# Gathering rows for the experts without their reciprocal root, and the first gather by bank

## What is computed

```python
hn = rms_norm(x, norm2_g[i])                       # x * rsqrt(mean(x*x) + eps) * g, row by row
x  = x + hier_moe(hn, ...)
# hier_moe: group = argmax(hn @ w_rg + b); two best of the 8 experts in that group, by hn @ w_re + b
#   for each expert e, its rows xb:  hdn = silu(xb @ w_gate[e]) * (xb @ w_up[e]);  y = hdn @ w_down[e]
#   x[row] += gate_weight[row, e] * y
```

## Time and profile before

| what | us |
|---|---|
| median of 3 runs | 1759.47 (1758.72 to 1763.71) |
| the profiled execution | 1758.96 |
| its span, first to last instruction | 1756.9 |
| first gather to the end of the experts, layer 0 | 435.7 to 880 |
| the same in layer 1 | 1307.6 to 1751 |

### The profile page before, as it was taken

How to read it: one execution, slowest core, us unless ns; L and a number is a source line. 1 busy time by engine, 2 the same in 40 slices (tenths; PEclk the granted TensorE clock), 3 DMA queues, 4 the chain that set the end, 5 groups by cost and what they waited for, 6 DMA issues and landing times.

```text
span 1756.9 us, 23311 instructions
## 1 busy us (share of the span) xinstructions
PE 1696.4 (97%) x9006; PEld 1062.0 (60%) x9006; DVE 719.3 (41%) x1341; ACT 683.0 (39%) x1541; POOL 667.5 (38%) x536
## 2 busy tenths in 40 slices
PE   8999999999999999899999999999999999998997
PEld 5889877787434444343378898777874444443443
DVE  5728788624222212121266387876241212222122
ACT  5565787754211111111156567877541111111111
POOL 6888776894000000000077987768930000000000
PEclk9999999999999999999999999999999999999999
DMA  6554312766999999999954452227569999999997
GB/s 252 209 184 153 144 49 102 291 278 239 365 417 425 427 426 426 426 425 428 414 223 161 180 192 97 94 100 313 220 250 413 427 426 425 426 426 427 426 423 303
DMA packets 52708, 528.48 MB, mean 301 GB/s; under 512 B 5704, under 2 KB 8520, under 8 KB 22384
## 3 DMA queue, kind: packets, MB, share of 16 engines
q1 hardware_dynamic: 52560, 526.89, 73.5%
q0 software_dynamic: 32, 0.02, 0.0%
HBM read 525.82 MB, written 1.06 MB: 300 GB/s over the span
## 4 chain that ended last, share of the span: by engine, by line
PE 65%; DMA 11%; DVE 9%; SPq 5%; ACT 4%; issue 3%; POOL 2%; DVEq 0%; ACTq 0%
PE PS L1274 18%; DMA view<-in_w_exp_down_dram 11%; PE PS L1303 9%; PE PS L858 8%; PE PS L860 8%; PE PS L859 8%; SPq L682 5%; DVE view L1954 5%; PE PS L1221 2%; POOL view L2321 2%; PE PS L1207 1%; PE PS L1065 1%; DVE view L1950 1%; PE PS L833 1%; ACT view L1527 1%
## 5 line engine op out<-in xcount | busy, mean ns | idle before, releaser
L2321 POOL TENSOR_TENSOR view<-view,view 128x512 fp32r<-128x512 f32 x448 | 579.1, 1316 | 555.9 <-DVE view L1856 466.8
L1274 PE MATMUL PS<-view,view 128*64 128x512 f32 x2048 | 454.6, 596 | 24.1 <-issue 23.3
L1415 ACT ACTIVATE view<-view 128x512 fp32r<-128x512 f32 x448 | 273.7, 630 | 152.8 <-PE PS L860 147.7
L1274 PEld LDWEIGHTS PS<-view,view 128*64 128x64 f32 x2048 | 153.6, 137 | 296.8 <-issue 293.5
L858 PE MATMUL PS<-view,view 128*128 128x512 f32 x704 | 285.2, 405 | 5.7 <-POOL view L2321 3.2
L860 PE MATMUL PS<-view,view 128*128 128x512 f32 x704 | 274.9, 390 | 0.0
L859 PE MATMUL PS<-view,view 128*128 128x512 f32 x704 | 274.7, 390 | 0.0
L1303 PE MATMUL PS<-view,stb 128*64 128x512 f32 x1024 | 230.3, 597 | 9.3 <-DMA view<-in_w_exp_down_dram 6.5
L2221 DVE SCALAR_TENSOR_TENSOR view<-PS,gcol,view 128x512 fp32r<-128x512 f32 x64 | 48.0, 750 | 447.6 <-ACT view L1723 447.5
L858 PEld LDWEIGHTS PS<-view,view 128*128 128x128 f32 x704 | 132.3, 188 | 33.5 <-issue 5.9
L1303 PEld LDWEIGHTS PS<-view,stb 128*64 128x64 f32 x1024 | 72.2, 136 | 132.6 <-issue 116.6
(11 more groups left out here) (254 smaller groups left out, 2034.5 us busy)
## 6 DMA issues: line engine op xcount, KB each, us to landing
view<-in_w_mix_dram SPq DMA_DIRECT2D x56, 2048.0 KB, 7.6
view<-in_w_exp_up_dram SPq DMA_DIRECT2D x54, 2048.0 KB, 27.6
view<-in_w_exp_gate_dram SPq DMA_DIRECT2D x50, 2048.0 KB, 28.2
view<-in_w_exp_down_dram SPq DMA_DIRECT2D x50, 2048.0 KB, 30.4
view<-in_w_exp_down_dram SPq DMA_DIRECT2D x44, 512.0 KB, 14.9
view<-in_w_exp_up_dram SPq DMA_DIRECT2D x28, 512.0 KB, 15.3
view<-in_w_exp_gate_dram SPq DMA_DIRECT2D x14, 1024.0 KB, 12.4
view<-in_w_exp_gate_dram SPq DMA_DIRECT2D x28, 512.0 KB, 25.9
```

The costliest lines, as they stand in the source:

```text
L1274: ins = pe.matmul(bank(ph, name, j)[e * CAP:(e + 1) * CAP, :], xgT1[:, k, at + e * CAP:at + (e + 1) * CAP], rows8(expert_block(j, kind, e) ...
L1415: nc.scalar.activation(highs(chunk), weights(slot8, chunk), ACT.Copy).then_inc(*high_ready.up(ph))
L2321: g_.tensor_tensor(weights(low8, chunk), weights(slot8, chunk), highs(chunk), ALU.subtract).then_inc(*low_ready.up(ph))
```

## The change

- ACT writes XNh as X rounded, without the root, one half of the columns at a time: columns 0 to 511 of both tiles after its work for n = 0, columns 512 to 1023 after its work for n = 1. The squares of n = 0 and 1 go to other scratch memory, since XNh now lies where they went.
- DVE writes the low part of columns 0 to 511 into a tile of its own, xl0, after n = 0; that of columns 512 to 1023 into XNl after `select(0)`; and once more that of columns 0 to 511 into XNl after the gates' weights, for the later gathers. Each is one tensor_tensor of 2 x 512 columns.
- The first gather runs bank by bank, 8 products each: banks 0 and 1 ahead of the gate product, bank 2 ahead of its k = 2, bank 3 ahead of its k = 4.
- `roots` makes the root of each place: a product of the selection (128 stationary columns, fp32) with the roots of the rows, one moving column, for two pairs and two tiles, so four products. For the first half they run ahead of the gate product into bank 4, for later halves behind the place weights in `turned_selection` of the odd pair before. ACT copies them to `rcol`.
- silu gets the root's column as its scale, and DVE's multiplication of up and silu becomes a scalar_tensor_tensor with the same column.
- The further passes get the same in their own form (not shown).

```diff
-        xnh_ready = sig("xnh_ready", 1, 0)
-        xnl_ready = sig("xnl_ready", TT, 0)
+        xnh_ready = sig("xnh_ready", 2, 0)
+        xnl_ready = sig("xnl_ready", 3, 0)
@@ PE, gather and first_gather
                     if i == 0:
                         pe.wait_ge(*S_ready.at(ph, h + 1))
+                        pe.wait_ge(*xnl_ready.at(ph, 3))
...
-                def first_gather(i, t, part):
-
+                def first_gather(i):
+
+                    pe.wait_ge(*xnh_ready.at(ph, 1 + i // 2))
+                    pe.wait_ge(*xnl_ready.at(ph, 1 + i // 2))
+                    pe.wait_ge(*free(ph, "xg", 0, i))
                     for k in (2 * i, 2 * i + 1):
...
+                        cols = slice(k * P, (k + 1) * P)
+                        for t in range(TT):
+                            for lower in range(2):
+                                rows = (xl0 if lower and i < 2 else XNl if lower else XNh)[:, t, cols]
+                                ins = pe.matmul(bank(ph, "xg", 0, i)[:, (k % 2) * HALF:(k % 2 + 1) * HALF],
+                                                rows, S2[0][:, t, :], start=(t == 0 and not lower),
+                                                stop=(t == TT - 1 and lower == 1))
+                    ins.then_inc(*fill(ph, "xg", 0, i))
+
+                def roots(o, h):
+
+                    for j in (2 * h, 2 * h + 1):
+                        at = (j % 2) * 2 * CAP
+                        for t in range(TT):
+                            ins = pe.matmul(o[:, j % 2:j % 2 + 1], S2[h % 2][:, t, at:at + P].bitcast(F32),
+                                            st[:, 64 + t:65 + t], start=(t == 0), stop=(t == TT - 1))
                     return ins
...
                 pe.wait_ge(*S_ready.at(ph, 1))
...
+                first_gather(0)
+                first_gather(1)
+                pe.wait_ge(*free(ph, "rc"))
+                roots(bank(ph, "rc"), 0).then_inc(*fill(ph, "rc"))
...
+                    if gathered(j):
+                        ins = roots(PS[:, 7, TT * P + 2:TT * P + 4], h + 1)
                     ins.then_inc(*fill(ph, "G", j))
...
                         for k in range(KD):
+                            if kind == 0 and j == 0 and k in (2, 4):
+                                first_gather(1 + k // 2)
                             if kind == 0 and j % 2 == 0 and k % 2 == 0:
                                 pe.wait_ge(*out_of(ph, "xg", h, k // 2))
@@ ACT
...
-                act.wait_ge(*r_ready.at(ph, 1))
-                act.wait_ge(*sumsq.made(ph))
-                for t in range(TT):
-                    ins = nc.scalar.activation(XNh[:, t, :], X[:, t, :], ACT.Copy, scale=st[:, 64 + t:65 + t])
-                ins.then_inc(*xnh_ready.up(ph))
+                    nc.scalar.activation(XNh[:, :, n * COLS:(n + 1) * COLS], X[:, :, n * COLS:(n + 1) * COLS], ACT.Copy
+                                         ).then_inc(*xnh_ready.up(ph))
...
-                for i in (0, 2):
-                    gathered_out(0, i)
...
+                gathered_out(0, 0)
+                roots_out(("rc",), bank(ph, "rc")[:, 0:2], rcol[:, 0:2])
+                gathered_out(0, 2)
...
-                nc.scalar.activation(silug, PS[:, 0, :], ACT.Silu).then_inc(*drain(ph, "g", j))
+                nc.scalar.activation(silug, PS[:, 0, :], ACT.Silu, scale=rcol[:, j % 4:j % 4 + 1]
+                                     ).then_inc(*drain(ph, "g", j))
@@ ACT, selection_out
+                if gathered(j):
+                    at = (j + 1) % 4
+                    ins = nc.scalar.activation(rcol[:, at:at + 2], PS[:, 7, TT * P + 2:TT * P + 4], ACT.Copy)
@@ DVE
+                def lower_rows(to, n, high_rows):
+
+                    cols = slice(n * COLS, (n + 1) * COLS)
+                    dve.wait_ge(*xnh_ready.at(ph, high_rows))
+                    v.tensor_tensor(to, X[:, :, cols], XNh[:, :, cols], ALU.subtract).then_inc(*xnl_ready.up(ph))
...
+                    if n == 0:
+                        lower_rows(xl0, 0, 1)
...
                 select(0)
-                dve.wait_ge(*xnh_ready.at(ph, 1))
-                for t in range(TT):
-                    v.scalar_tensor_tensor(out=XNl[:, t, :], in0=X[:, t, :], scalar=r_row[:, t:t + 1],
-                                           in1=XNh[:, t, :], op0=ALU.mult, op1=ALU.subtract
-                                           ).then_inc(*xnl_ready.up(ph))
+                lower_rows(XNl[:, :, COLS:], 1, 2)
...
                 gates()
+                lower_rows(XNl[:, :, 0:COLS], 0, 1)
...
-                v.tensor_tensor(hh, PS[:, 1, :], silug, ALU.mult).then_inc(*drain(ph, "u", j))
+                v.scalar_tensor_tensor(out=hh, in0=PS[:, 1, :], scalar=rcol[:, j % 4:j % 4 + 1], in1=silug,
+                                       op0=ALU.mult, op1=ALU.mult).then_inc(*drain(ph, "u", j))
```

More of the change, by code:

```diff
@@ L233, in unit_fills @@
 def unit_fills():
-    f = [(("xg", k), 5 + k % 3) for k in range(KD)]
+    f = [(("xg", k), 5 + k % 3) for k in range(KD)] + [(("rc",), 4)]
     for j in range(PAIRS):
@@ L374, in encoder @@
         XNh = view(r_w, TT, D, dt=F32R)
+        xl0 = view(r_v, TT, COLS, dt=F32R)
         sq = view(r_w, 2 * D)
@@ L1233, in first_gather @@
+                def roots(o, h):
[4 more added lines that the diff above has]
+                                            st[:, 64 + t:65 + t], start=(t == 0), stop=(t == TT - 1))
                     return ins
-                pe.wait_ge(*xnh_ready.at(ph, 1))
                 pe.wait_ge(*S_ready.at(ph, 1))
-                for i in range(4):
-                    pe.wait_ge(*free(ph, "xg", 0, i))
-                    for t in range(TT):
-                        first_gather(i, t, XNh)
@@ L1241, in first_pass @@
-                pe.wait_ge(*xnl_ready.at(ph, 1))
-                for i in range(4):
-                    first_gather(i, 0, XNl)
-                pe.wait_ge(*xnl_ready.at(ph, 2))
-                for i in range(4):
-                    first_gather(i, 1, XNl).then_inc(*fill(ph, "xg", 0, i))
+                first_gather(0)
+                first_gather(1)
+                pe.wait_ge(*free(ph, "rc"))
+                roots(bank(ph, "rc"), 0).then_inc(*fill(ph, "rc"))
                 def turned_selection(j):
@@ L1343, in unit @@
                     ins.then_inc(*fill(ph, "xg", k))
+                pe.wait_ge(*free(ph, "rc"))
+                for j in range(PAIRS):
+                    for t in range(TT):
+                        ins = pe.matmul(bank(ph, "rc")[:, j:j + 1], S[:, t, j * P:(j + 1) * P].bitcast(F32),
+                                        st[:, 64 + t:65 + t], start=(t == 0), stop=(t == TT - 1))
+                ins.then_inc(*fill(ph, "rc"))
                 for k in range(KD - 2, KD):
@@ L1632, in layer @@
                         act.wait_ge(*out_of(ph, "wo", n, t))
-                        nc.scalar.activation(sq[:, (2 * n + t) * COLS:(2 * n + t + 1) * COLS],
-                                             X[:, t, n * COLS:(n + 1) * COLS], ACT.Square,
+                        if n:
+                            act.wait_ge(*sumsq.at(ph, 14 + t))
+                        nc.scalar.activation(stb[:, :] if t else Lms[1], X[:, t, n * COLS:(n + 1) * COLS], ACT.Square,
                                              accum_out=small[:, 2 * n + t:2 * n + t + 1]).then_inc(*sumsq.up(ph))
@@ L1652, in gathered_out, with roots_out @@
                     ins.then_inc(*drain(ph, "xg", h, i))
-                for i in (0, 2):
-                    gathered_out(0, i)
+                def roots_out(key, rows, to):
+                    act.wait_ge(*full(ph, *key))
+                    nc.scalar.activation(to, rows, ACT.Copy).then_inc(*drain(ph, *key))
+                    act.wait_ge(*out_of(ph, *key))
+                gathered_out(0, 0)
+                roots_out(("rc",), bank(ph, "rc")[:, 0:2], rcol[:, 0:2])
+                gathered_out(0, 2)
                 act.wait_ge(*soft.at(ph, 4))
@@ L1744, in unit @@
                     scaled(ph, xgT[:, k, :], ("xg", k), G2 + k)
+                act.wait_ge(*full(ph, "rc"))
+                nc.scalar.activation(rcol[:, :], bank(ph, "rc")[:, 0:4], ACT.Copy).then_inc(*drain(ph, "rc"))
+                act.wait_ge(*out_of(ph, "rc"))
                 for j in range(PAIRS):
```

8 lines of the change are left out of this document (2 added, 6 removed).

## The result

Medians of 12 runs of each kernel on the same chip:

| what | before, us | changed, us |
|---|---|---|
| median | 1760.47 (1758.43 to 1763.71) | 1765.52 (1762.78 to 1767.43) |
| ratio, 95% interval | | 1.0028 (1.0020 to 1.0035) |
| the profiled execution | 1758.96 | 1766.88 |
| its span | 1756.9 | 1764.9 |

What follows compares the result with a forecast made beforehand. The prediction took the weight stream at 426 GB/s to bound the expert stage, its start set by the release behind pair 0's down product. It added +0.78 us a layer: 1758.96 + 2 x 0.78 = 1760.5 us, range 1757.0 to 1763.8.

Steps and rivals of the forecast that it cites:

- the sum: Path from first gather to pair 0's down product: 1.95 + 0.84 + 2.30 + 0.06 = 5.15 against 4.37, +0.78 us a layer.
- T: Point in the expert stage where the weight stream gets going for good: 464.7, set by the release at 463.34.
- theory F: From the follow-ups, not the prediction: TensorE's 3.49 us stand in layer 1's first transposes is instruction fetch, some 4.2 us in all.
- what I haven't seen, 0.01: Chance 0.01 kept for causes not named, with no place or size; counted under faster.
- B's one hand-off: TensorE stops once a layer inside the gate product for a bank's copy, 1.14 us: 1762.8.
- D: Roots and bank 0's copy hold the first gate product to 440.1: 1.6 us more a layer, 1763.7; chance 0.03.
- the release term: Load behind pair 0's down product released at 464.1 instead of 463.34: +0.78 us a layer.
- The earlier loads: First quarter load 1.8 us earlier in the gate product, twelve loads ending at 462.7, not 464.7; gain ends as idle queue.
- The rest of the hiding: ACT's and DVE's moved copies lie beside other work at no cost; tightest is bank 3's copy, 0.8 us in hand.
- rival B: TensorE waits for bank copies inside the gate product: 1762.8 for one a layer, 1767.3 for all three; chance 0.12.
- The roots' price: Eight records ahead of the gate product, 0.087 us each, upper bound 0.122: 0.70 to 0.98, middle 0.84 taken.
- The base: Profiled execution of the kernel before, 1758.96 us, to which 2 x 0.78 was added.

Runs made afterwards that it cites:

- the place put back: Changed kernel plus 91 instructions in a branch never executed, layer 1's first instruction back at place 18 of 256: 1761.22 us (1.0011); repeated, 1761.56 (1.0007).
- the place moved alone: Kernel before plus 165 instructions in a branch never executed, layer 1's first instruction moved from place 18 to 183: 1764.56 us, 1.0033.
- hold ahead of pair 0's down product: Kernel before with ten short keep-busy products (2.2 us) ahead of pair 0's down product in each layer, place kept: 1762.95 us, 1.0017.
- hold behind the first gather: Kernel before with ten short keep-busy products between the first gather and pair 0's gate product, place kept: 1762.42 us, 1.0017.
- the three products: Three bf16 products in the wait ahead of the last row transposes, place 18: kernel before 1758.60 us (0.9996), repeated 1758.93 (0.9995); changed kernel 1759.58 (1.0000).

## Why the prediction was wrong

**The failed step** is the one that isn't in the sum. I priced every instruction that is executed on the way to T and between pairs, and held the rest of the program for unchanged. TensorE's program is 165 instructions longer ahead of the target of a jump that is taken 445 us behind the first gather, and by theory F a block's end came to lie 14 instructions behind that target. That stand, with the slower clock behind it, is 4.2 us in the profiles (431.50 - 427.34), 4.3 by the runs with the place put back (1765.52 - 1761.22, medians of two comparisons with their own kernel before; by the ratios to it, 1.0028 less 1.0009, 3.3), and 5.4 by the runs with the place moved alone (1764.56 - 1759.16). It was among "what I haven't seen, 0.01". None of the rivals had it; that B's one hand-off and D end near 1763 is chance.

**The sum itself.** With the place put back, the change costs +1.6 us (1.0009; 2.1 and 2.5 by the medians), and +1.56 was forecast. That the two agree so well is partly luck: two of the sum's parts were off, with opposite signs. Point by point, from the first gather's start:

| step | forecast | measured |
|---|---|---|
| start of the gate product | 2.79 | 2.91 |
| of it 16 gather records | 1.95 | 2.03 |
| of it 8 records of roots | 0.84 | 0.88 |
| gate and up products with two inserts | 16.27 | 16.54 |
| up product to down product | 2.23 | 2.25 |
| release behind the down product, against before | +0.78 | +1.20 |
| end of the stage, against before | +0.78 | +0.94, +0.72 |
| end of the loads ahead of the release | 27.0 | 28.9 |
| stream lost behind them, in us of 426 GB/s | 2.8 | 1.4 |

Each insert cost 1.15 in the chain, as taken from the earlier trace rows, but the product's pieces of 8 records took 1.87 instead of 1.75: leaving and entering the product costs 0.1 again beside the insert. The rest of the 0.42 is the gather's and the roots' 0.12 and less than 0.1 in small pieces. So the release term was mis-sized by half.

The second error has the other sign: I took a microsecond at the release for a microsecond of the weight stream. The windows from 4 to 33 us behind the start of the first gather, one a layer, say how much of a later release the stream feels (mean GB/s in layer 0 and 1, and what is missing against the kernel before in us of 426 GB/s):

| kernel | release later by | GB/s | stream behind by |
|---|---|---|---|
| before | | 337, 340 | |
| changed | 1.20 | 328, 327 | 0.61, 0.88 |
| hold ahead of pair 0's down product | 2.26 | 312, 312 | 1.70, 1.91 |
| hold behind the first gather | 1.80 | 317, 317 | 1.36, 1.57 |

Some 0.2 to 0.6 us of the delay doesn't reach the stream, for a short delay as for a long one. The ends of the stages say the same. Over the six profiles without a hold ahead of T of the kernel before they have means of 444.77 and 442.46 us; over the four of the changed kernel with its inserts and roots, 445.53 and 443.25. That is +0.77 and +0.79, with single profiles up to 0.7 us from their mean. So T follows the release, but for the first few tenths, as if the loads ahead of it still had bytes on the way then. That this is the reason is argued, not shown: the hold behind the first gather puts those loads off as well and loses a few tenths too.

**The earlier loads** gained nothing, as forecast, but not for the whole of the reason given. I had the twelve loads end 2 us earlier and the queue then wait. They ended at 28.9 us from the gather, no earlier than before. Quarters that are released one at a time, with inserts in between, leave holes: 291 GB/s in 453 to 454 above, where the earlier trace rows has 426. Behind them the queue never stood idle for a whole microsecond: the 262, 188 and 221 GB/s from 466 to 469 are 1.4 us of the stream lost, less than the 2.8 us of idle queue that were forecast, since the loads were late, not early.

**The rest of the hiding** came as worked out. ACT's silu with its scale column takes 0.69 and DVE's product 0.75, as taken from the earlier trace rows. DVE's copy of bank 3, the tightest, begins at once and is 0.88 long, and TensorE doesn't wait for it (timelines of ACT and DVE in the changed kernel):

```profile
450.45 0.69 ACT L1719 ACTIVATE view<-PS,rcol 128x512 f32<-128x512 f32 x1 [2.80 <-PE PS L1289]
```

```profile
446.86 0.88 DVE L2183 TENSOR_SCALAR view<-PS,vcol 128x256 f32<-128x256 f32 x2 [5.94 <-PE PS L1239]
...
457.32 0.75 DVE L2244 SCALAR_TENSOR_TENSOR view<-PS,rcol,view 128x512 f32<-128x512 f32 x1 [5.11 <-PE PS L1289]
```

So rival B is out: no hand-off shows in the gate. Rival D is out: the gate product starts 1.5 us earlier. Two pairs' period is 54.07 us in the chain of the changed kernel, for 53.18, +0.89 where 0.96 was forecast:

```profile
486.68 3.58 PE PS L1318 x16
...
540.75 3.58 PE PS L1318 x16
```

**The roots' price**: 0.88 us from the first of eight records to the next product, 0.11 each, where the earlier trace rows gave 0.087 and, as the upper bound, 0.122. The Trainium skill's 25 ns, given there for a product of so few columns by itself ("TensorE: Matmul & The Clock Gate", Back-to-back issue gap) isn't what the row shows; its price by stationary columns (LDWEIGHTS, 107 ns) is.

**The base** was 1.5 us low (1758.96, for a median of 1760.47), within what the runs scatter. The profiled execution of the kernel before had no fall of the clock near 430 and 1302; that of the changed kernel had one. Whole runs seem to show it as a lower mean clock: over the four later comparisons the runs of the kernel before at a mean clock of 0.997 or more have a median of 1758.9 us, and those below it 1761.3. 37 of these 107 runs of the kernel before are of the second sort, 14 of 24 of the changed kernel at the old place, and 5 of 34 of the kernels with the three products. That the change makes the fall more frequent is possible, and part of its 1.6 us may be that; the counts don't settle it.

## What to carry to other kernels

Before an edit of a program with a jump in it is priced, ask what it does to the place of everything behind it: a change of length alone, in code that never runs, moved this kernel by 0.3%, as much as any mechanism here. When a trace shows an engine standing still with no releaser, look at the same instruction in the kernel before and at the instruction queue, and pad to the old place before the change is blamed or praised. And a transfer that may start earlier is worth nothing while a later release sets when the stream runs unbroken.

## What the runs showed of the hardware

- Behind a jump, TensorE stood for 3.49 and 3.86 us after 14 instructions; with the code placed 26 instructions further from there, for 0.47 us after 40; and with 179 by the same count, not at all. By theory F these are the distances from the jump's target to the next block's end. The instruction queue's second packet came 5.5 to 6 us after the first in each of the three with a stand, and TensorE went on 2.7 to 2.9 us after it.
- A stand of 3.5 us was followed by a granted clock of 0.58 and 0.57 for some 3 us, mostly the level of 1.2 GHz. The stand of 0.47 us was not.
- Around 430 us, where a wait of 0.83 us is followed by products of 36 columns, the clock fell in 8 of 22 layers of like kernels. The 20 keep-busy products then took 5.7 to 6.0 us instead of 4.48. Runs of the kernel before with a mean clock under 0.997 had a median 2.5 us above the others'; that the falls make this difference is likely, not shown run by run.
- Of a release of the weight loads that came 1.20 and 2.26 us later, the stream of weights lost 0.61 and 0.88, 1.70 and 1.91 us.
- Leaving a chain of fp32 products for another form of operand cost about 0.1 us beyond the inserted records (segments of 8 records at 1.87 us instead of 1.75).
